# An FFN with seven block products for eight: moved from the down projection to the up projection, with plain down pairs woven between

## The reference, cut to what matters

```python
uv = jnp.einsum('bld,df->blf', h, w_up)            # w_up: 1024 x 5632
u, gate = uv[..., :D_FF], uv[..., D_FF:]
u_ext = jnp.concatenate([conv_prev, u], axis=1)
uc = conv_b + sum(conv_w[j] * u_ext[:, j:j + seq] for j in range(CONV_W))
y = jnp.einsum('blf,fd->bld', jax.nn.gelu(uc, approximate=False) * gate, w_down)
```

## Time and profile before

| | us |
|---|---|
| median of 3 runs | 1604.25 (1603.68 to 1604.71) |
| profiled execution | 1609.08 |
| its span, first to last instruction | 1607.1 |
| TensorE busy in it | 1571.3 |
| VectorE busy in it | 1101.5 |
| ScalarE busy in it | 707.8 |
| GpSimd busy in it | 601.8 |

### The profile page before, as it was taken

How to read it: one execution, slowest core, us unless ns; L and a number is a source line. 1 busy time by engine, 2 the same in 40 slices (tenths; PEclk the granted TensorE clock), 3 DMA queues, 4 the chain that set the end, 5 groups by cost and what they waited for, 6 DMA issues and landing times.

```text
span 1607.1 us, 40959 instructions
## 1 busy us (share of the span) xinstructions
PE 1571.3 (98%) x17831; PEld 1530.0 (95%) x17831; DVE 1101.5 (69%) x1747; ACT 707.8 (44%) x1174; POOL 601.8 (37%) x394
## 2 busy tenths in 40 slices
PE   8999999999999999999999999999999999999997
PEld 7999989899999999999999999888999999999997
DVE  4679656675778677856647894566667786787664
ACT  5545356553334333433454644556433343334334
POOL 5345422223344343434333453122234434343331
PEclk9999999999999999999999999999999999999999
DMA  5222210012322322232332222000223232323222
GB/s 157 66 80 79 66 43 4 4 35 83 88 80 73 99 80 88 83 94 74 89 96 74 72 79 74 10 4 4 60 80 90 81 92 80 92 66 105 83 73 90
DMA packets 219123, 115.42 MB, mean 72 GB/s; under 512 B 9588, under 2 KB 216706, under 8 KB 218946
## 3 DMA queue, kind: packets, MB, share of 16 engines
q1 hardware_dynamic: 218866, 112.79, 24.7%
q10 hardware_dynamic: 80, 0.02, 0.0%
HBM read 109.27 MB, written 3.53 MB: 70 GB/s over the span
## 4 chain that ended last, share of the span: by engine, by line
PE 89%; DVE 5%; issue 2%; DMA 2%; POOL 1%; ACT 1%; SPq 0%; DVEq 0%; ACTq 0%
PE ps L758 31%; PE ps L759 31%; PE ps L1335 3%; PE ps L1337 3%; PE ps L1336 3%; PE ps L1008 2%; PE ps L1011 2%; PE ps L1005 2%; DMA raw<-in_ffn_w_down 1%; DVE Tall L2603 1%; PE ps L970 1%; POOL wlo L731 1%; PE ps L982 1%; PE ps L1073 1%; PE ps L763 1%
## 5 line engine op out<-in xcount | busy, mean ns | idle before, releaser
L635 POOL TENSOR_TENSOR wlo<-raw,whi 128x1024 fp32r<-128x1024 f32 (+1 forms) x169 | 432.3, 2558 | 621.2 <-ACT whi L1436 621.2
L1436 ACT ACTIVATE whi<-raw 128x1024 fp32r<-128x1024 f32 (+1 forms) x170 | 176.6, 1039 | 384.1 <-PE ps L759 359.4
L758 PE MATMUL ps<-xh,whi 128*128 128x288 f32 x1120 | 331.7, 296 | 1.8 <-DVE xl L2017 1.8
L759 PE MATMUL ps<-xh,whi 128*128 128x288 f32 x1120 | 329.4, 294 | 0.0
L758 PE MATMUL ps<-xl,whi 128*128 128x288 f32 x1120 | 329.3, 294 | 0.0
L759 PE MATMUL ps<-xl,whi 128*128 128x288 f32 x1120 | 329.3, 294 | 0.0
L758 PE MATMUL ps<-xh,wlo 128*128 128x288 f32 x1120 | 329.1, 294 | 0.0
L759 PE MATMUL ps<-xh,wlo 128*128 128x288 f32 x1120 | 328.8, 294 | 0.0
L758 PEld LDWEIGHTS ps<-xh,whi 128*128 128x128 f32 x1120 | 210.2, 188 | 3.8 <-issue 3.1
L759 PEld LDWEIGHTS ps<-xh,whi 128*128 128x128 f32 x1120 | 210.2, 188 | 0.2
L759 PEld LDWEIGHTS ps<-xl,whi 128*128 128x128 f32 x1120 | 210.2, 188 | 0.0
(11 more groups left out here) (370 smaller groups left out, 3628.9 us busy)
## 6 DMA issues: line engine op xcount, KB each, us to landing
raw<-in_ffn_w_up SPq DMA_DIRECT2D x88, 512.0 KB, 3.8
raw<-in_w_in SPq DMA_DIRECT2D x52, 512.0 KB, 3.8
raw<-in_ffn_w_down SPq DMA_DIRECT2D x32, 512.0 KB, 4.0
raw<-in_w_out SPq DMA_DIRECT2D x16, 512.0 KB, 4.1
raw<-in_ffn_w_down SPq DMA_DIRECT2D x16, 384.0 KB, 3.4
xin<-in_x_prompt SPq DMA_DIRECT2D x4, 512.0 KB, 7.1
out<-xin SPq DMA_DIRECT2D x8, 256.0 KB, 2.9
out<-RW SPq DMA_DIRECT2D x16, 64.0 KB, 2.2
```

The source lines that it names most:

```text
L635: e.tensor_tensor(wlo[s][:, 0:width], raw[s][:, 0:width], whi[s][:, 0:width].bitcast(F32), ALU.subtract).then_inc(w_lo[s], 1)
L758: e.matmul(acc(out)[:, 0], lhsT, rhs[:, 0:HT], start=start, stop=stop)
L759: return e.matmul(acc(out)[:, 1], lhsT, rhs[:, HT:TOK], start=start, stop=stop)
L1436: e.activation(whi[s][:, 0:width], raw[s][:, 0:width], ACT.Copy).then_inc(w_hi[s], 1)
```

## The change

In each layer the parts of h become 2, 4, 4, 4, 4 and 4 tiles.

- Up: pair 0 is plain (96 matmuls). Pairs 1 to 21 are block products (`folded_up`, 84 matmuls each). The 2 by 2 blocks are now the even and odd tiles of x by the two halves of the tokens. The mixed columns `Xhi`, `Xlo` of x are made once a layer while the output projection runs (ScalarE `xpair` and `mix_hi`, VectorE `mix_tokens` and `mix_lo`). The weight sums, splits and GpSimd's three low parts are per pair, as they were per folded down pair, now 21 times a layer for 8.
- The two outputs of a pair come out of four PSUM banks: copies `copy_b`, `move_v`, `copy_c` on ScalarE, sums and scaling on VectorE.
- Down: all plain. Behind each up pair f >= 2 stands one pair of output tiles for an earlier part (`mixed_products`), with 2 or 4 input tiles: 24 or 48 matmuls. Its weights go through buffers of their own, with high parts on ScalarE (`down_hi`) and low parts on VectorE (`down_rest`). `add_down` adds the result into x. The last part's four pairs are as before, with 4 input tiles for 6.

VectorE's stream in one round, with ScalarE's beside it:

```diff
+                def folded_up(f):
+                    if f >= 3:
+                        add_down(*mixed_down(f - 1), 1)
+                    if more:
+                        for name in SUMS:
+                            quad_sum(f + 1, name)
+                    if f >= 2:
+                        down_rest(*mixed_down(f), 1)
+                    pad(f)
+                    dv.wait_ge(d_prod, nth(PE_D, m, "P2"))
+                    e.tensor_tensor(up[:, 2:2 + DEC], bank_a[:, 0:DEC], nrs[:, 0:DEC], ALU.mult)
+                    e.tensor_tensor(up[:, 4 + DEC:4 + HT], bank_a[:, DEC:HT], nrs[:, DEC:HT], ALU.mult).then_inc(u_add, 1)
+                    if f >= 2:
+                        down_rest(*mixed_down(f), 0)
+                    if more:
+                        quad_lo(f + 1, "S2")
+                    dv.wait_ge(d_copy, nth(AC_C, m, "v"))
+                    dv.wait_ge(d_prod, nth(PE_D, m, "P7"))
+                    e.tensor_tensor(hf[:, HT:TOK], bank_b, vs[:, :], ALU.add).then_inc(u_add, 1)
+                    added_up(f, "c22")
+                    e.tensor_tensor(hf[:, HT:TOK], hf[:, HT:TOK], nrs[:, HT:TOK], ALU.mult).then_inc(u_add, 1)
+                    dv.wait_ge(d_prod, nth(PE_D, m, "P3"))
+                    e.tensor_tensor(up[:, 4 + HT:4 + TOK], bank_c, vs[:, :], ALU.add).then_inc(psum_free[0], 1)
+                    dv.wait_ge(psum_free[0], own[0])
+                    e.tensor_tensor(up[:, 4 + HT:4 + TOK], up[:, 4 + HT:4 + TOK], nrs[:, HT:TOK], ALU.mult).then_inc(u_add, 1)
+                    added_up(f, "u12")
+                    keep_last(f)
+                    if more:
+                        quad_lo(f + 1, "S3")
+                    dv.wait_ge(tile_done[1], own[1])
+                    e.tensor_tensor(hf[:, 0:HT], bank_b, nrs[:, 0:HT], ALU.mult).then_inc(psum_free[1], 1)
+                    if more:
+                        quad_lo(f + 1, "S4")
+                    conv_rest(f)
+                    if f >= 2:
+                        add_down(*mixed_down(f), 0)
+                    if more:
+                        quad_lo(f + 1, "S1")
+                    gated(f, -1.0)
+                    inner_lo(f)
...
+                for f in range(1, FF):
+                    more = f + 1 < FF
+                    copy_b(f)
+                    if more:
+                        quad_hi(f + 1, "A11")
...
+                    if f >= 2:
+                        down_hi(*mixed_down(f), 1)
+                    move_v(f)
+                    if f >= 2:
+                        down_hi(*mixed_down(f), 0)
+                    copy_c(f)
+                    if more:
+                        for name in ("S2", "A12", "S3", "S4"):
+                            quad_hi(f + 1, name)
...
+                    conv_first(f)
+                    if more:
+                        quad_hi(f + 1, "A22")
+                    gelu(f)
+                    if more:
+                        quad_hi(f + 1, "S1")
+                    inner_hi(f)
```

On TensorE (`product` is 12 matmuls), and the start of the FFN on ScalarE and VectorE:

```diff
+                def folded_up(f):
...
+                    product(f, "P1", bank_a, True)
+                    product(f, "P5", bank_v, True)
+                    pe.wait_ge(d_copy, nth(AC_C, m, "b"))
+                    product(f, "P6", bank_b, False)
+                    product(f, "P2", bank_a, False)
+                    pe.wait_ge(d_copy, nth(AC_C, m, "c"))
+                    product(f, "P7", bank_b, False)
+                    product(f, "P3", bank_c, False)
+                    pe.wait_ge(u_add, nth(DV_U, m, "c22"))
+                    product(f, "P4", bank_b, False)
...
+                quad_hi(1, "A11")
+                for name in ("S2", "S3", "S4"):
+                    quad_hi(1, name)
+                conv_first(0)
+                quad_hi(1, "A12")
+                quad_hi(1, "A22")
+                gelu(0)
+                quad_hi(1, "S1")
+                inner_hi(0)
...
+                    for name in SUMS:
+                        quad_sum(1, name)
+                    conv_rest(0)
+                    for name in ("S2", "S3", "S4"):
+                        quad_lo(1, name)
                     dv.wait_ge(tile_done[1], t1)
...
+                    e.tensor_tensor(by_half(hf[:, :]), acc(PS[1]), by_half(nrs[:, :]), ALU.mult).then_inc(psum_free[1], 1)
+                    quad_lo(1, "S1")
+                    gated(0, 1.0)
+                    inner_lo(0)
```

More of the change, by code:

```diff
@@ new lines, in _ @@
+                load_up(0)
+                load_up(1)
+                for f in range(1, FF):
+                    if f >= 2:
+                        load_down(*mixed_down(f))
+                    if f + 1 < FF:
+                        load_up(f + 1)
+                sp.wait_ge(d_sum, nth(SUMS, folded(l, FF - 1), "S4"))
+                for it in range(KT // 2):
+                    for s in range(2):
+                        load(s, turn(s, l, PAIRS["ffn"] + FF + it),
+                             raw[s][:, 0:DW].rearrange("p (k m) -> p k m", m=P), down_rows(MIXED, it, s))
@@ new lines, in mixed_products @@
+                def mixed_products(g, it):
+                    q, n = down(l, g, it), PARTS[g]
+                    hi, lo = hh[:, slots(g)], hl[:, slots(g)]
+                    for s in range(2):
+                        pe.wait_ge(e_lo[s], q + 1)
+                        pe.wait_ge(e_free[s], q)
+                        for kt in range(n):
+                            if it == 0 and s == 0:
+                                pe.wait_ge(f_dve, (l * FF + F_AT[g] + kt + 1) * len(F_DV))
+                            wh, wl = (down_weights(w, s, n, kt) for w in (whi_all, wlo_all))
+                            for lhsT, rhs, first, last in ((wh, hi[:, kt], kt == 0, False), (wh, lo[:, kt], False, False),
+                                                           (wl, hi[:, kt], False, kt == n - 1)):
+                                mm = both(PS[2 + s], lhsT, rhs, first, last)
+                        mm.then_inc(e_done[s], 1)
@@ L1457, in spare_split, with mix_hi, added @@
                 e.activation(spare_hi[:, :], raw[0][:, 0:KT * P], ACT.Copy).then_inc(w_hi[0], 1)
[L1459 removed]
+            def mix_hi(l, it):
+                ac.wait_ge(xm_done, (l * FH + it + 1) * 4)
+                e.activation(Xhi[:, :, it], xmix[:, :, :], ACT.Copy).then_inc(xm_hi, 1)
+            def added(l, pair, c, width, after, rows=False, ready=False, mix=False):
                 for k in range(KT):
@@ L1478, in added @@
                         square(c, k)
+                    if mix and k >= 2 and s == 0:
+                        mix_hi(l, it - 1)
+                    if mix and s == 1:
+                        ac.wait_ge(xm_done, (l * FH + it) * 4)
+                        for i in range(2):
+                            e.activation(xpair[:, i], x[:, k - 1 + i, :], ACT.Copy, scale=gain(c, k - 1 + i)).then_inc(xp_done, 1)
                     if rows and k == 2:
@@ new lines, in quad_hi @@
+                def quad_hi(f, name):
+                    k = [turn(s, l, PAIRS["ffn"] + f - 1) + 1 for s in range(2)]
+                    if f == 1 and name in ("A11", "S1"):
+                        ac.wait_ge(tile_done[0], k[0])
+                    elif f == 1 and name in ("A12", "A22"):
+                        ac.wait_ge(tile_done[1], k[1])
+                    elif f == 1:
+                        ac.wait_ge(xm_lo, (l + 1) * FH)
+                    elif name == "S1" and f > 2:
+                        ac.wait_ge(e_done[0], down(l, *mixed_down(f - 1)) + 1)
+                    elif name == "S1":
+                        ac.wait_ge(tile_done[0], k[0])
+                    elif name == "A22":
+                        ac.wait_ge(tile_done[1], k[1])
+                    else:
+                        reader = dict(A11="P1", A12="P2", S2="P6", S3="P7", S4="P3")[name]
+                        ac.wait_ge(d_prod, nth(PE_D, folded(l, f - 1), reader))
@@ L1961, in widen_tile, with gelu @@
                      .then_inc(f_cv, 1)
-                    if fold:
-                        quad_hi(g - 1, 0, "A12")
-                        quad_hi(g - 1, 0, "A22")
-                        first_copy(g - 1, 0)
+                def gelu(f):
+                    t = l * FF + f
                     ac.wait_ge(f_dve, t * len(F_DV) + F_DV.index("c2") + 1)
                     e.activation(gl[:, :], cv[:, :], ACT.Gelu).then_inc(f_gelu, 1)
-                    if not fold:
-                        tile(1, k[1], width)
-                        inner_hi(g, it)
@@ L2739, in _ @@
+                plain_up()
+                for f in range(1, FF):
+                    folded_up(f)
+                add_down(*mixed_down(FF - 1), 1)
+                add_tiles(PAIRS["ffn"] + FF, (l + 1) * NORMS)
             dv.wait_ge(y_rs, 2)
```

581 lines of the change are left out of this document (243 added, 338 removed).

## The result

The changed kernel takes 1629.74 us (median of 4 runs, 1628.07 to 1630.95), the kernel before beside it 1604.48 (4 runs, 1603.68 to 1605.42): a ratio of 1.0157, 95% interval 1.0139 to 1.0174. It is slower, by 25.3 us where I had forecast 9.2. 1629.74 lies at the upper end of the forecast's own range, 1601 to 1630.

What follows compares the result with a forecast made beforehand. TensorE bounds the kernel before; VectorE, held up by GpSimd, was to set the new rounds. Matmuls of 385.2 us plus stalls gave 418.9 for 414.3 a layer, 9.2 slower in two: 1613.5 us, range 1583 to 1643 (forecast's own 1601 to 1630).

Steps and rivals of the forecast that it cites:

- out tile to end of first c22: FFN start, from the last output projection tile's addition to the first c22: 29.9 us, including a 7.5 us P5 stall.
- step from c22 1 to 2: Round from f = 1 to 2, without down additions: 16.85 us for TensorE's 11.1, so 5.75 us of stall.
- four rounds of two: Rounds with n = 2 down input tiles: 17.15 us each for TensorE's 14.27, 11.6 us of stall over four.
- the rest, 15 steps and the last tiles: Rounds with n = 4 at 17.95 us for 17.44, 7.5 us of stall over 15, and an FFN end costing nothing.
- The walk through VectorE's stream: VectorE's work in an n = 4 round, walked in order: 15.1 us without GpSimd, 17.95 with its hits.
- The three hits: GpSimd's low parts of A22, A11 and A12 delay VectorE each round by 1.0, 0.85 and 1.1: together 2.9 us.
- The stall ahead of the first P5: FFN start: TensorE waits 7.5 us for S1's low part, since P1 ends at 405.0.
- The late load: Rival: the sums wait for their DMA load, 1632 us, or 1643 to 1650 with another wait; chance 0.25 including more waits.
- The halved and the missing conflict: Two rivals: GpSimd's hits half as large, 1581 to 1598.5 us, chance 0.22; no hits at all, 1565 us, chance 0.06.
- the terms for the FFN's start and for f = 1 to 2: Stalls per layer: 7.5 us at the first P5 plus 0.35 for copy_b, and 5.75 for the round f = 1 to 2.
- It lags by well under 1 us: FFN end, 24-matmul tiles 3.17 us apart: VectorE needs 3.2 each, so its lag over 8 tiles costs nothing.
- the 0.5 us a round: Rounds with n = 4: TensorE stalls 0.5 us ahead of P4, VectorE's 17.95 for TensorE's 17.44.

Runs made afterwards that it cites:

- e2: Changed kernel with GpSimd's three low parts (A11, A12, A22) cut from 128x512 to 128x32, the rest not computed; 1586.54 us.
- e3: Changed kernel with the two low parts of the down weights per round moved from VectorE to GpSimd; 1659.25 us.
- e5: Changed kernel with S1's parts made first in the first two folded rounds of each FFN, and scaling and copy of P1 earlier; 1622.3 us.
- e7: Changed kernel with the orders of e5 and e6 together, same instructions; 1601.39 us.
- e1: Changed kernel with 52 and 28 small idle matmuls ahead of P5 in rounds f = 1 and 2 of each layer; 1617.13 us.
- e4: Changed kernel with ScalarE's high part of S1 placed ahead of the gelu instead of behind it; 1616.14 us.
- e10: Changed kernel with only VectorE's two low parts (down slot 0 and S2) moved behind the making of c22; 1619.58 us.
- e6: e4 with VectorE's two low parts (down slot 0 and S2) also moved behind the making of c22; 1602.54 us.
- e11: Against e7, first two folded rounds: ScalarE's copies ahead of later work, VectorE's c22 ahead of the next round's sums; 1598.72 us, ratio 0.9974.

## Why the prediction was right or wrong

By its own steps, in us, with layer 1 in brackets where it differs:

| step | predicted | measured | miss |
|---|---|---|---|
| out tile to end of first c22 | 29.9 | 32.5 [31.1] | +2.6 [+1.2] |
| step from c22 1 to 2 | 16.85 | 18.6 [17.8] | +1.8 [+1.0] |
| four rounds of two | 68.7 | 69.5 | +0.8 |
| the rest, 15 steps and the last tiles | 303.5 | 304.7 [304.9] | +1.2 [+1.4] |
| sum | 418.9 | 425.3 [423.3] | +6.4 [+4.4] |

The 29.9 are 156 matmuls up to P7 (20.6), 1.0 for the norm, 7.5, 0.35 and c22 itself (0.45); the 303.5 are the other 2244 matmuls (296.4) and 7.5, less that 0.45.

**Right.** The direction and its reason: 20.6 us of matmuls a layer are given up again by VectorE, which GpSimd holds up (e2, e3). The walk through VectorE's stream gave 17.95 and the chip 17.98; for n = 2 it gave 17.15, the chip 17.23 in three of the four rounds. The three hits were put at 0.85, 1.1 and 1.0 and measure 0.9, 1.1 and 1.0. The stall ahead of the first P5 was put at 7.5 and is 7.39, and P5 starts 22.6 us after the out tile, as forecast. The late load is refuted for the changed kernel: the DMA released VectorE in the folded rounds only once, in round 1, with 0.21 us (in e5 and e7, where the start is earlier, it is 1.3 and 1.0). The halved and the missing conflict are refuted by the three hits. Some of the agreement is luck: the step to the last folded round is 16.8, not 17.95, and hides 1.2 us of what the end of the FFN cost.

**Wrong: the size, 9.2 for 25.3.** The mechanism held; the step that failed is the price of the matmuls behind a forecast stall, with smaller terms beside it:
- *The clock.* I priced every matmul at 0.1321 us, a row from a stretch without long stalls, and in the same sum forecast a stall of 7.5 us. After it they start 0.24 us apart. It is the terms for the FFN's start and for f = 1 to 2 that were mis-sized by it, by 3.9 us in layer 0 and 1.3 in layer 1, as e1 shows. My 16.85 was 0.5 too much for a step at full clock (16.36 in e1).
- *The first c22.* With the clock kept up it ends at 30.85 and 31.2 (e1), 0.9 and 1.3 later than my terms have it. It stands behind S2's low part, and that is the one that GpSimd's A12 hits; my terms for the start have no hit between P5 and c22.
- *Rounds of two.* 0.8 a layer: the last of the four steps is 17.77.
- *The base.* The sum went against 414.3 for both layers. Layer 1 of the kernel before is 413.1, which I had not read: 1.2.
- *The end.* "It lags by well under 1 us" failed: in layer 0 the last tile's addition comes 4.71 us after the one before it, where the tiles before are 3.17 apart. VectorE's low part of x ahead of it is hit by GpSimd's (changed kernel, VectorE, then GpSimd):

```profile
811.29 2.31 DVE L2071 SCALAR_TENSOR_TENSOR xl<-x,gains,xh 128x576 fp32r<-128x576 f32 x1 [1.06 <-ACT xh L1474]
```
```profile
810.60 2.40 POOL L660 TENSOR_TENSOR wlo<-raw,whi 128x1024 fp32r<-128x1024 f32 x1 [2.31 <-ACT whi L1464]
```

That is 1.5 in layer 0. In layer 1 the last addition is 1.75 late, but there VectorE waits for TensorE, and the kernel before has the same 1.75 (6.51 for 4.76): it belongs to both. The lag of layer 0 costs the next layer little: its last scaled tile `Tall` starts 102.7 us after the last addition, 102.3 before, and 101.8 to 102.7 in all thirteen traces.

The account of the FFNs closes: 9.2 forecast, 6.4 + 4.4 of misses and 1.2 of base are 21.2 us, the difference of the FFN lengths. The medians differ by 25.3, with an interval of 22.3 to 27.9 by the ratio; what lies between is outside the FFNs, or chance, and stays open.

**Half right: what the 0.5 us a round was.** I took the round for VectorE's whole stream with its hits and priced it well, and the rows of the changed kernel bear that out: VectorE never waits for TensorE in the equal rounds of four. What I had not seen is that 1.7 us of that stream hang on the order. e4, e10 and e6 have all of VectorE's instructions; with both edits a wait of 0.61 for ScalarE goes and one hit of 1.1 falls where it costs nothing, and TensorE's stall is gone in the rounds of four. In the rounds of two "VectorE is too slow" stays true, 16.54 for 14.3 in e6. VectorE is busy for 300.0 of 330 us in the rounds, 91%, and 87% in the whole FFN, where I had said near 80: the records hold the time in which it is blocked.

## What to carry to other kernels

When a change forecasts a stall of some microseconds on TensorE, price the matmuls behind it at both levels of the clock; in these runs that was worth 5 us, and filling the stall with idle matmuls got it back. Where engines feed each other in rounds, walk every ring (what the next product waits for, and what stands ahead of that in its engine's queue) and don't stop at adding up an engine's work: here some 25 us hung on the place of three instructions in a round. Look where a hit by another engine falls, on work or on a wait. And follow a removed stall into the next queue before promising its length: at the FFN's start it moved three times, from e6 to e11, and gave 4.2 us of FFN length.
